# Score passes over half the partitions, two units back to back, in a decoder layer's attention

## What is computed

```python
# 8 stick-breaking heads (4 groups of 2), head width 64
z = einsum('bhqd,bhkd->bhqk', q[:, :, start:end], k[:, :, :end]) * scale
log_beta = log_sigmoid(z)
log_1m_beta = where(mask, log_sigmoid(-z), 0.0)
suffix = cumsum(log_1m_beta, axis=3, reverse=True) - log_1m_beta
a = where(mask, exp(log_beta + suffix), 0.0)
out = einsum('bhqk,bhkd->bhqd', a, v[:, :, :end])

# 4 differential heads (4 groups), two score maps of width 64 each
p1 = softmax(where(mask, z1, -inf)); p2 = softmax(where(mask, z2, -inf))
out = einsum('bhqk,bhkd->bhqd', p1 - lam * p2, v[:, :, :end])
```

## Time and profile before

| | us |
|---|---|
| median of three runs (lowest, highest) | 1483.84 (1483.18, 1483.91) |
| profiled execution, span | 1482.4 |
| attention groups 0 to 7, from the first scores on | 49 to about 660 |
| of these, stick-breaking / differential | 49 to 426 / 426 to 660 |
| PE busy, share of the span | 1467.3, 99% |
| DVE busy | 989.1, 67% |
| ACT busy | 666.5, 45% |
| POOL busy | 359.8, 24% |
| mean granted TensorE clock | 0.998 of full speed |

### The profile page before, as it was taken

How to read it: one execution, slowest core, us unless ns; L and a number is a source line. 1 busy time by engine, 2 the same in 40 slices (tenths; PEclk the granted TensorE clock), 3 DMA queues, 4 the chain that set the end, 5 groups by cost and what they waited for, 6 DMA issues and landing times. The chain is left out here.

```text
span 1482.4 us, 19461 instructions
## 1 busy us (share of the span) xinstructions
PE 1467.3 (99%) x7188; PEld 1223.9 (83%) x7188; DVE 989.1 (67%) x1236; ACT 666.5 (45%) x1037; POOL 359.8 (24%) x280
## 2 busy tenths in 40 slices
PE   9999999999999999999999999999999999999997
PEld 8888888887888888888888888888888888888886
DVE  3776776768857557454456788766664477568767
ACT  3555554556556556442032245444443534433343
POOL 2635445455444234211240040000000000000004
PEclk9999999999999999999999999999999999999999
DMA  5111112111101101121452225544442688845563
GB/s 181 58 29 58 58 43 65 63 57 44 57 30 56 30 15 42 29 58 57 139 202 71 92 94 172 183 157 156 156 157 100 213 302 287 291 138 191 191 198 134
DMA packets 111648, 172.41 MB, mean 116 GB/s; under 512 B 6096, under 2 KB 71888, under 8 KB 111440
## 3 DMA queue, kind: packets, MB, share of 16 engines
q1 hardware_dynamic: 111568, 171.33, 34.1%
HBM read 127.27 MB, written 44.04 MB: 116 GB/s over the span
## 5 line engine op out<-in xcount | busy, mean ns | idle before, releaser
L759 PE MATMUL p_proj<-xt_h,w_hi 128*128 128x512 f32 x640 | 254.0, 397 | 0.6 <-DVE xt_l L1613 0.6
L763 PE MATMUL p_proj<-xt_h,w_lo 128*128 128x512 f32 x640 | 252.7, 395 | 0.0
L761 PE MATMUL p_proj<-xt_l,w_hi 128*128 128x512 f32 x640 | 251.1, 392 | 0.0
L2314 POOL TENSOR_TENSOR w_lo<-w_raw,w_hi 128x512 fp32r<-128x512 f32 x96 | 134.7, 1424 | 216.3 <-DVE w_hi L1621 215.7
L2433 POOL TENSOR_TENSOR row_odd<-row_odd,gains 128x1024 f32<-128x1024 f32 x4 | 10.4, 2620 | 578.7 <-ACT row_odd L1585 578.7
L763 PEld LDWEIGHTS p_proj<-xt_h,w_lo 128*128 128x128 f32 x640 | 120.3, 188 | 23.7
L759 PEld LDWEIGHTS p_proj<-xt_h,w_hi 128*128 128x128 f32 x640 | 120.4, 188 | 22.7 <-DVE xt_l L1613 0.6
L761 PEld LDWEIGHTS p_proj<-xt_l,w_hi 128*128 128x128 f32 x640 | 120.5, 188 | 20.6
L1613 DVE TENSOR_TENSOR d_al<-f_a,d_ah 128x1024 fp32r<-128x1024 f32 x56 | 68.5, 1224 | 78.7 <-ACT d_ah L1502 78.6
L1502 ACT ACTIVATE d_ah<-f_a 128x1024 fp32r<-128x1024 f32 x56 | 59.2, 1057 | 133.6 <-PE p_av L1149 54.9
L1350 ACT ACTIVATE a_t<-p_tr 128x384 fp32r<-128x384 f32 (+3 forms) x96 | 47.2, 492 | 123.3 <-PE p_tr L861 123.1
(11 more groups left out here) (297 smaller groups left out, 3529.1 us busy)
## 6 DMA issues: line engine op xcount, KB each, us to landing
f_a<-h_terms SPq DMA_DIRECT2D x56, 512.0 KB, 3.4
w_raw<-w_in SPq DMA_DIRECT2D x40, 512.0 KB, 3.9
h_terms<-c SPq DMA_DIRECT2D x40, 512.0 KB, 3.4
f_b<-w_ff SPq DMA_DIRECT2D x40, 512.0 KB, 5.0
r<-w_ff SPq DMA_DIRECT2D x32, 512.0 KB, 3.9
gate_rows<-gst SPq DMA_DIRECT2D x12, 512.0 KB, 5.1
y<-x SPq DMA_DIRECT2D x8, 512.0 KB, 8.0
wo_raw<-w_out SPq DMA_DIRECT2D x8, 512.0 KB, 9.8
```

The lines of the kernel that those rows point to most:

```text
L759: pe.matmul(o, w_hi[n_slot][:, k, :], xt_h[:, k, cols], start=(k == 0), stop=False)
L761: pe.matmul(o, w_hi[n_slot][:, k, :], xt_l[:, k, cols], start=False, stop=False)
L763: mm = pe.matmul(o, w_lo[n_slot][:, k, :], xt_h[:, k, cols], start=False, stop=(k == KT - 1))
L2314: low = pool.tensor_tensor(w_lo[slot][:, ks, :], w_raw[:, ks, :], w_hi[slot][:, ks, :].bitcast(F32), ALU.subtract)
```

## The change

A new function, `score_pair(g, j, masked)`, gives the units j (m = 0) and j + 1 (m = 1) of one query block together. First come all passes with the keys' high part of m = 0, then of m = 1. Then come the passes with the keys' low part, chunk by chunk, m = 0 and m = 1 in turn, and each over its own 64 partitions alone: partitions 0 to 63 for m = 0, 64 to 127 for m = 1. `qk_done` rises for both units behind their last low pass.

- In every group units 0 and 1 come as a pair.
- Stick-breaking groups: units 2 and 3 come as a pair at `fill_to(12)` (unit 3 stood behind turn 0), and then a pair (u + 3, u + 4) stands behind each turn with b == 0 and odd u; behind even u there are no scores. All 16 units are paired.
- Differential groups: units 2 and 3 come as a pair at `fill_to(24)`, between the two rounds of value transposes (unit 2 stood at `fill_to(12)`). Units 2u + 4 and 2u + 5 come as a pair for u = 0 to 3, where they stood together before; for u = 4 and 5 (query blocks 6 and 7) they stay as they were, by the old function.

The other engines' programs are unchanged, and so is the number of matmuls.

```diff
+            def score_pair(g, j, masked):
+
+                qb = j // 2
+                width = (qb + 1) * P
+                lhs = [q_st[m][:, qb * P:(qb + 1) * P] for m in range(2)]
+                rr = [slice(HD * m, HD * m + HD) for m in range(2)]
+                for m in range(2):
+                    if not (isinstance(g, int) and g == 0 and j < 2):
+                        pe.wait_ge(z_read, g * 16 + (j - 1 + m))
+                    for lo in range(0, width, NH):
+                        w = max(min(width - lo, NH), 256)
+                        pe.matmul(p_z[m][:, lo:lo + w], lhs[m], k_hi[m][:, lo:lo + w], start=True, stop=False)
+                        if masked and lo + NH >= width:
+                            pe.matmul(p_z[m][:, qb * P:width], ident_r[:, :], later_r[:, :], start=False, stop=False,
+                                      skip_group_check=True)
+                for lo in range(0, width, NH):
+                    w = max(min(width - lo, NH), 256)
+                    for m in range(2):
+                        mm = pe.matmul(p_z[m][:, lo:lo + w], lhs[m][rr[m], :], k_lo[m][rr[m], lo:lo + w],
+                                       start=False, stop=True)
+                        if lo + NH >= width:
+                            mm.then_inc(qk_done, 1)
+
             def first_scores(g, masked):
...
-                scores(g, 0, masked)
-                scores(g, 1, masked)
+                score_pair(g, 0, masked)
...
                 fill_to(12)
-                scores(g, 2, not G.sb)
+                if G.sb:
+                    score_pair(g, 2, False)
                 fill_to(18)
...
                     if vb == 0:
                         fill_to(24)
                         if not G.sb:
-                            scores(g, 3, True)
+                            score_pair(g, 2, True)
...
                     if G.sb:
-                        if b == 0 and u + 3 < G.nunits:
-                            scores(g, u + 3, False)
+                        if b == 0 and u % 2 and u + 3 < G.nunits:
+                            score_pair(g, u + 3, False)
                     elif u + 2 < G.nunits:
...
-                        if b == 0:
+                        if b == 0 and last_b:
+                            score_pair(g, 2 * u + 4, True)
+                        elif b == 0:
                             scores(g, 2 * u + 4, True)
-                        if last_b:
+                        elif last_b:
                             scores(g, 2 * u + 5, True)
```

## The result

The changed kernel takes **1505.33 us** (median of four runs, 1504.23 to 1507.29) against 1483.88 before: a ratio of 1.0144, 95% interval 1.013 to 1.0159. It is slower by 21.5 us, where 8.6 were forecast, and lies 0.3 us outside the range.

The account below looks back on a forecast made before the run. The prediction took TensorE's own sequence as the bound. Paired passes -10.4, row changes +9.0, differential heads +7.0 and stick-breaking turns +3 gave +8.6 us on 1483.84, so 1492.4 us, range 1480 to 1505.

Parts of the forecast that it names:

- What bounds the kernel: Whole kernel: TensorE's own sequence is the time, PE busy 99% of the span, with 3.0 us of waits.
- Term 1: Paired low passes: the two halves run side by side, saving 10.4 us, with 0 and 13.9 as bounds.
- the floor of two weight loads: Paired low passes: a pair can't be shorter than two loads, 0.212 us, unless the loads overlap too.
- Term 2: Changes between 128 and 64 rows around pairs: 112 at 0.08 us each, +9.0 us.
- the rival with the emptied array: Row changes: the array runs empty at each, costing 18 to 30 us; total 1501 to 1513 us, chance 0.18.
- Term 3: Differential groups' heads: TensorE waits before value transpose round 1, 1.75 us in each of four groups, +7.0 us.
- Term 4: Stick-breaking groups' turns: the wait for VectorE in unit 12 grows by up to 0.91 us each, +3 us taken.
- The hope for a shorter scan: Stick-breaking turns: VectorE's scan might shorten from 3.41 us, as it takes 2.10 elsewhere; lower bound 0.
- The faster rival: Pairs: row changes cost under about 0.02 us and both passes run at once; 1477 to 1484 us, chance 0.25.
- The one in which passes run one behind the other: Paired low passes: 64-row passes don't overlap and save nothing; 1494 to 1503 us, chance 0.19.

Follow-up runs that it names:

- e14: Changed kernel with both low passes of each pair over partitions 0 to 63, so none runs beside the other half: 1515.84 us.
- e4: Kernel before, in its own order, with each low pass over its own 64 partitions and no partner: 1548.99 us.
- e9b: Changed kernel with low passes over all 128 rows and ScalarE's round 0 value copy in eight pieces, lengthening the head waits: 1501.25 us.
- e10: Changed kernel with two projection matmuls moved behind the differential groups' pair of units 2 and 3, shortening the head waits: 1499.19 us.
- e5: Kernel before with only the stick-breaking groups' scores in the changed places, unpaired and over 128 rows: 1487.58 us.
- e6: Changed kernel with each pair's low passes ordered all m = 0, then all m = 1, instead of chunk by chunk: 1505.77 us.
- e12: Kernel before with one filler table entry moved, putting some two more projection matmuls between unit 12's turns in stick-breaking groups: 1481.23 us.
- e3: Kernel before with the differential groups' units 2 and 3 moved directly ahead of value transpose round 1, unpaired, over 128 rows: 1490.36 us.
- e1: Changed kernel's order with the low passes over all 128 rows again: 1495.21 us.

## Why the prediction was wrong

**What bounds the kernel** was read rightly: every part of the loss lies on TensorE's own sequence or its waits.

**Term 1** forecast -10.4 us and kept 13.9 as its end; e14 shows 13.1, or some 13.6 without its shorter waits. The step that failed is the floor of two weight loads, taken from loads that all used the same rows: loads of the two halves overlap. The Trainium skill, "TensorE: Matmul & The Clock Gate" (Part 3), has the second matmul of another row group almost free; the trace agrees with it (0.49 us for the two passes, 0.50 for one alone in e4), and not with my floor.

**Term 2** forecast +9.0 us at 0.08 per change; it is 0.18 to 0.20 (e4, and the rows of the pair), some 20 us for 112 changes. This is the term that was sized worst. The step that failed is taking the middle between no cost and an emptied array, and leaving the uncovered load, 0.11, to the end of the range alone. The array doesn't run quite empty (0.09 us beyond the stream, where the prediction had 0.16 for an emptied one), but the load adds its whole length on each side. "TensorEngine Tiling (Array Packing)" of the Trainium skill (Tiling Modes, Key Properties) says that a change of mode drains the engine; e4 agrees that it costs, 0.17 to 0.20 us a change, and the rule pointed at the rival with the emptied array, which I gave 0.18. Terms 1 and 2 together: -1.4 forecast, +5.8 measured.

**Term 3** forecast +7.0 us of waits; they are 6.6. The mechanism held, and the chain's price to 0.15 us per head (1.60 and 1.69 against 1.75). What failed is the sentence that TensorE loses the wait alone: behind most idle stretches of 1.6 to 2.0 us its clock was granted at half, 1.6 us more each time. This is 4.8 us in the profiled run, and no rival had it. e9b and e10 show it to be the idle time's doing.

**Term 4** forecast +3; e5 gives 3.6, the upper bound. The hope for a shorter scan didn't come true.

So 8.6 forecast and 21.5 measured differ by 7.2 from terms 1 and 2, 4.8 from the clock and small sums. The time is that of the rival with the emptied array (1501 to 1513), and its mechanism, a costly change of rows, is what was found; but it is in part luck that the number fell there. Without the clock's 4.8 us it would be 1500.5, below that rival's range and inside mine; with half clock behind two heads, as in e6's profile, 1503.7, inside both. The faster rival failed at its first condition, the change's cost under 0.02 us. The one in which passes run one behind the other is refuted by e14.

## What to carry to other kernels

Matmuls over half of the rows come free beside a partner in the other half, but entering and leaving them costs 0.2 us each time. A pass of 512 columns takes 0.23 us, so about two such passes must run free behind one entry before it breaks even; such work should be gathered in long runs or left alone. Before moving work, ask whether it leaves TensorE idle in one long piece: gaps up to 1.3 us cost their own length here, while behind most gaps of 1.6 to 2.0 us in the changed kernel, e6 and e9b the clock cost as much again. And a short wait that stands in the waits view is worth filling: the one taken apart in e12 cost 0.46 us beyond the 0.38 shown, and one entry of a table mended it.

## What was not expected of the hardware

- Half clock (1.2 instead of 2.4 GHz) behind idle times of 1.6 and 1.7 us (changed kernel, three of four heads; e6, two of four) and of 1.9 and 2.0 us (e9b, three of four), with none in the profiled executions with 1.0 (e10) and 1.3 us (e3). Waits of 1.48 to 1.58 us in e1 and e14 brought none in the profiles either, but one of e14's other runs has a mean clock of 0.996 instead of 0.998 or 0.999 and is 1.3 us above the median. Where exactly it begins, and why waits of equal length end differently, stays open.
- Two 64-row passes of different halves overlap whole, loads included, in either order of issue; a pass that waits for its own half is overtaken by one of the other half (e6).
- The load of the first pass after a change isn't run ahead: it starts with its pass.
